# Block 2 of a two-block model on one core: the two output-gate projections of each head pair in seven quarter products

## The chip, the cores and the metric

One core of a Trainium2 chip runs the whole program in one launch. The metric is device time in microseconds (us); lower is better. All data is float32.

## The reference

Two transformer-like blocks run one after the other on 256 tokens of width 1024. The change lies in the second one, in the projection of the normed input `h` and in what follows for two of its parts:

```
h = _rmsnorm(x, norm_g[l]) * (1.0 + scale[:, None, :]) + shift[:, None, :]
p = jnp.einsum('bsd,de->bse', h, w_in[l])
c_val, c_gate, c_og, ts, r_og, g_conv, g_rwkv = jnp.split(p, SPLITS, axis=-1)
y_conv = _conv_branch(c_val, c_gate, c_og, ...)   # ends: silu(u) * silu(og)) @ w_o
y_rwkv = _rwkv7_branch(ts, r_og, ...)             # ends: (o * silu(og)) @ w_o
m = jax.nn.sigmoid(g_conv) * y_conv + jax.nn.sigmoid(g_rwkv) * y_rwkv
x = x + gate[:, None, :] * jnp.einsum('bsd,de->bse', m, w_out[l])
```

`c_og` and `r_og` are the output gates of the convolution and of the recurrence, `g_conv` and `g_rwkv` the branch gates; each is 1024 wide. The recurrence `_rwkv7_scan` runs over 16 heads of width 64.

## The kernel before

**Layout.** `hT` holds the normed input, transposed: 8 tiles `k` of 128 features by 256 tokens. The heads go two by two: 8 pairs of 128 columns. Each pair needs nine projections of 1024x128 weights, and each of these sits in its own slot of SBUF (`slot[w]`, 512 KB a load, issued on SP's queue by `load_projection`): `VAL`, `GATE`, `K_`, `R_`, `V_` (the list `NEXT`), and `OGP`, `ROG`, `GCP`, `GRP` (the list `OWN`: output gate of the convolution, of the recurrence, and the two branch gates). A plain projection (`projection`, L1015) is 8 matmuls of 128x256, accumulated into half a PSUM bank. Successive projections alternate between bank 0 and bank 1, and `read_out` makes each wait until the one two places before it in the same bank has been read.

**Seven products.** The two branch gates of pairs 0 to 6 are computed together (`own_gate_pair`, L1041). The two slots and `hT` are taken as 2x2 blocks (two slots by two halves of the features, and those by two halves of the tokens), and seven products of sums of blocks replace the eight products of blocks. Each is 4 matmuls of 128x128. The sums of `hT`, `bt`, are made once; the sums of the weights are made for each pair by VectorE in four steps of 128x512 (`slice_sum(0)` to `(3)`, L2601, L2604, L2607, L2610); three of them need room of their own (`bs`), one is made in place. The products land as seven quarters in the two banks; ScalarE copies one out (L1792), and VectorE adds the others to it (`first_quarter`, L2615, and `other_quarters`, L2622, L2625, L2627).

**Sections.** Block 2 runs in sections 0 to 8. Section `j` builds the chunk matrices of pair `j` (`grown`, L1186, and `inverted`, L1198 and L1200, five levels each), and at the same time takes the recurrence of pair `j - 1` through its four chunks (`forced`, L1135 and L1137; `solved`, L1145; `outcome`, L1158 to L1172). These are chains of small matmuls in which TensorE and VectorE alternate: `solved(c)` waits until VectorE has copied the result of `forced(c)` out (the copy F{c}, L2554), `outcome(c)` waits for the copy of `solved(c)` (U{c}, L2558), `inverted(l)` waits for the masked copy of `grown(l)` (G{l}, L2572), and the next level waits for VectorE's transpose of `inverted(l)` (L2578; L2585 for the last). To cover these waits, TensorE gets large matmuls between the chains: a generator (`behind`) yields the projections in small steps, and a written table says how many steps each place takes.

```
FILL = (0, 12, 11, 12, 11, 13, 13)
FILL_FIRST = (14, 9, 9, 10, 10, 10, 10)
```

A step is one matmul of 128x256, or two of 128x128 in the seven products. In section `j` of 0 to 6 the steps are, in this order: `NEXT` of pair `j + 1` (40 steps), `OGP` and `ROG` of pair `j` (16), the branch gates of pair `j` (14), 70 in all. The text calls the places fill 0 to fill 6 after their place in the table (fill 0 is empty in `FILL`; the last fill takes what is left, 11 of its 13). Fill 1 stands behind `solved(0)`, fill 2 behind `inverted(1)`, fill 3 behind `inverted(2)`, fill 4 behind `inverted(3)` (in two pieces, with the matmul for the key lengths, `kk.sum`, between them), fill 5 behind `inverted(4)`, fill 6 behind `inverted(5)`.

**VectorE's order.** All of VectorE's work is one list in program order: the copies of the chains, the operands of the next pair (`shift`, L2451; `operand_kp`, L2463; `operand_k`, L2468; `kk_lengths` with its reciprocal, L2474; `operand_b`, from L2478), the 31 taps of the convolution (L2511), the group norm of pair `j - 2` (its reciprocal L2519, in sections 2 to 7), the sums for the branch gates, and the two output gates: `og_silu` (L2589) and `rg_silu` (L2593) multiply a tanh made by ScalarE (L1720) with the projection, which they read from PSUM.

```
e.wait_ge(*act.upto(f"og.th.{j}"))
e.scalar_tensor_tensor(out=OG[:, j, :], in0=OG[:, j, :], scalar=1.0, in1=proj(OGP, j), ...)
```

`shift` of the keys waits for ScalarE's copies of the `K_` projection (L1670, L1672).

Of the kernel before, what the change touches and what calls it, by code (L numbers as in the profile page):

```python
# [110 lines left out]

FILL = (0, 12, 11, 12, 11, 13, 13)
FILL_FIRST = (14, 9, 9, 10, 10, 10, 10)
FILL_LAST = (0, 6, 5, 5, 5, 5, 6)
FILL_END = (0, 3, 3, 2, 3, 3, 3, 3, 3, 3, 3, 3, 2)

# [29 lines left out]
def build(nc, a, out):  # L148

    with ExitStack() as ctx:  # L150
# [869 lines left out]
        def gate_banks_of(q):  # L1020

            return [view3(bank[PLACE[w, q] % 2][:, :], P) for w in (GCP, GRP)]

        def own_gate_pair(e, q):

# [73 lines left out]
        def behind(e, j):  # L1099

            if j < LAST:
                for w in NEXT:
                    yield from projection(e, w, j + 1)
                for w in (OGP, ROG):
                    yield from projection(e, w, j)
                yield from own_gate_pair(e, j)
            elif j == LAST:
                yield from projection(e, OGP, j)
                yield from projection(e, ROG, j)
                yield from layer_sum(e, LNSUM, CU)  # L1110
# [594 lines left out]
        def act_rwkv(e, j):  # L1705
# [65 lines left out]
            if more:  # L1771
                if j:
                    act_pad(e, "v", V_, j + 1)
                half_gate(OGP, OG[:, j, :], "og.th", j)
            if levels:
                inverted(4)
            if more:
                half_gate(ROG, rg[j % 3], "rg.th", j)
            if levels:
                e.wait_ge(*pe.upto(f"tok.{j}"))  # L1780
                e.activation(tokBK[j % 2], chunks(bank[4][:, :]), ACT.Copy).then_inc(*act.step(f"tok.{j}"))
            if last:
                e.wait_ge(*pool.upto("ln.c0"))
                e.activation(lnq[:, 0:4, :], CU[:, 0:4, :], ACT.Square).then_inc(*act.step("ln.sq0"))
                e.wait_ge(*dve.upto("ln.c1"))
                e.activation(lnq[:, 4:8, :], CU[:, 4:8, :], ACT.Square).then_inc(*act.step("ln.sq"))
# [761 lines left out]
        def dve_rwkv(e, j):  # L2548
# [37 lines left out]

            def og_silu():
                e.wait_ge(*act.upto(f"og.th.{j}"))
                e.scalar_tensor_tensor(out=OG[:, j, :], in0=OG[:, j, :], scalar=1.0, in1=proj(OGP, j), op0=ALU.add, op1=ALU.mult).then_inc(*dve.step(f"og.{j}"))  # L2589

            def rg_silu():
                e.wait_ge(*act.upto(f"rg.th.{j}"))
                e.scalar_tensor_tensor(out=rg[j % 3], in0=rg[j % 3], scalar=1.0, in1=proj(ROG, j), op0=ALU.add, op1=ALU.mult).then_inc(*dve.step(f"rg.{j}"))  # L2593

            def slice_sum(k):

# [62 lines left out]
                e.tensor_tensor(Mt[j % 2], chunks(bank[6][:, T:]), each(cst2_of("st")), ALU.mult).then_inc(*dve.step(f"M.{j}"))  # L2659
                turned(1)  # L2660
            if more:
                slice_sum(0)
                dve_decays(e, j + 1)
            if levels:
                taps(e, j, *((23, 28) if not j else (27, CONV2) if more else (22, 27)))
            if j and more:
# [14 lines left out]
            if levels:  # L2681
                turned(2)
            if more:
                slice_sum(1)
                slice_sum(2)
                shift(e, "k", j + 1)
                operand_kp(e, j + 1)
            if j == 0:
                taps(e, j, 28, CONV2)
                join_taps(e, j)  # L2690
                conv_input(e, j + 1)
                taps(e, j + 1, 0, 2)
            elif more:
                taps(e, j + 1, 4, 10)
# [24 lines left out]
            if more:  # L2719
                shift(e, "r", j + 1)  # L2720
                bonus_keys(e, j + 1)
                taps(e, j + 1, *((10, 13) if j else (2, 6)))
                kk_lengths(e, j + 1)
            if last:
                rg_silu()
            if end:
# [10 lines left out]
            if levels:  # L2737
                turned(4)
            if more:
                slice_sum(3)  # L2740
                og_silu()
                operand_b(e, j + 1)
                shift(e, "v", j + 1)
                operand_a(e, j + 1)
                if not chain:
                    taps(e, j + 1, 6, 10)
# [510 lines left out]
        def sp_rwkv(e):  # L3257

            free = {R_: f"down{LATE}", K_: f"down{LATE}", VAL: f"down{BY_PRODUCT - 1}", V_: f"down{BY_PRODUCT - 1}",
                    GATE: "down.p1", ROG: "down.p1", GRP: "down.p5", OGP: "down.p3", GCP: "down.p3"}  # L3260
            summed = {R_: LATE, K_: LATE, VAL: BY_PRODUCT - 1, V_: BY_PRODUCT - 1, GATE: BY_PRODUCT, ROG: DOWN - 2,
                      OGP: BY_PRODUCT, GCP: DOWN - 2}

            def load_projection(w, j):
                e.wait_ge(*pe.upto(f"p{GRP if w == GCP else w}.{j - 1}" if j else free[w]))
# [164 lines left out]
```

## Time and profile before

| what | value |
|---|---|
| median of the timed runs | 1058.26 us (3 runs, 1057.3 to 1058.48) |
| the profiled execution's own time | 1057.9 us |
| span of the profile | 1055.9 us |
| TensorE busy | 1045.8 us |
| VectorE busy | 754.8 us |
| ScalarE busy | 237.4 us |
| sections 2, 3 and 4, from one `forced(0)` to the next | 46.6 us each |

Times in the rows are counted from the start of the span. Float32 matmuls leave two records each, so a row with x24 is 12 matmuls. The time from the start of one row to the start of the next on the same engine is what an instruction takes up; the duration shown is longer, since the end of an instruction lies beside the start of the next.

### The profile page before, as it was taken

To read this page: it belongs to the slowest core of one execution; us is meant where nothing else is said; L and a number is where in the kernel's file an instruction comes from. 1 tells how busy PE (TensorE), PEld (TensorE's weight loads), DVE (VectorE), ACT (ScalarE), POOL (GpSimd) and SP (SyncE) were. 2 spreads that over 40 slices of the span, in tenths; PEclk is the share of its full clock that TensorE was granted. 3 is DMA by queue.
4 is the path that set the end of the run, shared out by engine and by line. 5 is a ranking of instruction groups with operands and counts; after the bars stand their busy time and mean duration, and the time that the engine had idled before them with its cause. 6 is when DMAs were issued, how large, how long until landed. Compare 5 with 4: busy or idle time off the path is not lost.

```text
span 1055.9 us, 21666 instructions
## 1 busy us (share of the span) xinstructions
PE 1045.8 (99%) x8902; PEld 904.3 (86%) x8902; DVE 754.8 (71%) x1714; ACT 237.4 (22%) x630; POOL 121.0 (11%) x166
## 2 busy tenths in 40 slices
PE   9999999999999999999999999999999999999997
PEld 8899899998988499999644988898898989887983
DVE  4488776867743477777757788767878778777875
ACT  4032222213300120011101432323223232324101
POOL 1101000000045121100250000000000000000052
PEclk9999999999999999999999999999999999999999
DMA  8786666552377446554555333333333322161261
GB/s 271 260 308 234 208 197 220 194 186 86 120 228 230 159 71 251 195 190 162 182 194 220 99 102 101 99 103 101 105 102 97 120 82 80 42 241 41 81 160 40
DMA packets 72307, 162.67 MB, mean 154 GB/s; under 512 B 18929, under 2 KB 33169, under 8 KB 72210
## 3 DMA queue, kind: packets, MB, share of 16 engines
q1 hardware_dynamic: 71202, 159.67, 46.1%
q8 instruction: 71, 1.16, 0.4%
q10 hardware_dynamic: 1008, 1.63, 0.4%
q14 instruction: 26, 0.21, 0.1%
HBM read 160.17 MB, written 1.11 MB: 153 GB/s over the span
## 4 chain that ended last, share of the span: by engine, by line
PE 97%; DVE 1%; DMA 1%; issue 0%; ACT 0%; POOL 0%; DVEq 0%; ACTq 0%; POOLq 0%
PE bank L860 27%; PE bank L1015 18%; PE bank L491 13%; PE bank L926 6%; PE bank L1041 4%; PE bank L677 3%; PE bank L792 2%; PE bank L835 2%; PE bank L1186 2%; PE bank L1198 2%; PE bank L1355 2%; PE bank L988 1%; PE bank L1077 1%; PE bank L994 1%; PE bank L569 1%; PE bank L1055 1%
## 5 line engine op out<-in xcount | busy, mean ns | idle before, releaser
L1015 PE MATMUL bank<-hT,slots 128*128 128x256 f32 x896 | 204.5, 382 | 0.0
L1015 PEld LDWEIGHTS bank<-hT,slots 128*128 128x128 f32 x896 | 167.8, 190 | 23.2 <-issue 0.3
L860 PE MATMUL bank<-hT,slots 128*128 128x128 f32 x832 | 103.5, 276 | 0.0
L2511 DVE SCALAR_TENSOR_TENSOR arena<-padA,par,arena 128x256 f32<-128x256 f32 x232 | 102.8, 504 | 0.0
L860 PEld LDWEIGHTS bank<-hT,slots 128*128 128x128 f32 x832 | 97.9, 192 | 0.8 <-issue 0.7
L860 PE MATMUL bank<-arena,slots 128*128 128x128 f32 x768 | 95.6, 275 | 0.0
L860 PEld LDWEIGHTS bank<-arena,slots 128*128 128x128 f32 x768 | 90.9, 192 | 0.5
L491 PE MATMUL bank<-hT,slots 128*128 128x256 f32 x336 | 74.4, 380 | 0.0
L491 PEld LDWEIGHTS bank<-hT,slots 128*128 128x128 f32 x336 | 63.4, 190 | 9.2 <-issue 0.8
L491 PE MATMUL bank<-arena,slots 128*128 128x256 f32 x304 | 66.3, 380 | 0.5 <-DMA slots<-in_w_br 0.5
L491 PEld LDWEIGHTS bank<-arena,slots 128*128 128x128 f32 x304 | 57.5, 190 | 8.8 <-DMA slots<-in_w_br 1.1
L926 PE MATMUL bank<-slots,arena 128*128 128x512 f32 x128 | 55.4, 592 | 0.0
L926 PEld LDWEIGHTS bank<-slots,arena 128*128 128x128 f32 x128 | 24.2, 190 | 30.1 <-issue 25.6
L3052 POOL TENSOR_TENSOR arena<-arena 128x256 f32<-128x256 f32 x8 | 5.8, 728 | 359.8 <-ACT arena L1726 359.8
L860 PE MATMUL bank<-x,arena 128*128 128x128 f32 x352 | 46.5, 275 | 0.0
L860 PE MATMUL bank<-x,slots 128*128 128x128 f32 x352 | 46.5, 275 | 0.0
L860 PEld LDWEIGHTS bank<-x,slots 128*128 128x128 f32 x352 | 42.8, 192 | 0.0
L860 PEld LDWEIGHTS bank<-x,arena 128*128 128x128 f32 x352 | 42.8, 192 | 0.0
L1983 DVE SCALAR_TENSOR_TENSOR adaA<-arena,sc,adaA 128x1024 f32<-128x1024 f32 x24 | 30.7, 1277 | 0.0
L1595 ACT ACTIVATE arena<-bank 128x128 f32<-128x128 f32 x20 | 5.5, 277 | 110.2 <-PE bank L860 98.9
L2981 POOL TENSOR_TENSOR arena<-arena 128x256 f32<-128x256 f32 x8 | 8.0, 1020 | 188.8 <-DMA arena<-cum_scratch 188.8
L2168 DVE SCALAR_TENSOR_TENSOR arena<-arena,bank 128x256 f32<-128x256 f32 x32 | 12.6, 415 | 22.9 <-PE bank L491 15.8
(478 smaller groups left out, 1887.5 us busy)
## 6 DMA issues: line engine op xcount, KB each, us to landing
slots<-in_w_rwkv SPq DMA_DIRECT2D x72, 512.0 KB, 3.6
slots<-in_w_heads SPq DMA_DIRECT2D x64, 512.0 KB, 4.5
slots<-in_w_gu SPq DMA_DIRECT2D x44, 512.0 KB, 4.5
arena<-in_ada_w SPq DMA_DIRECT2D x24, 512.0 KB, 5.5
slots<-in_w_down SPq DMA_DIRECT2D x20, 512.0 KB, 4.4
slots<-in_w_br SPq DMA_DIRECT2D x32, 256.0 KB, 2.8
slots<-in_w_out SPq DMA_DIRECT2D x16, 512.0 KB, 4.2
slots<-in_w_y SPq DMA_DIRECT2D x16, 512.0 KB, 6.5
```

What stands on the lines that cost most here:

```text
L491: end = e.matmul(psum, w[:, k * P:(k + 1) * P], rhs[:, k, :], start=k == 0, stop=k == kt - 1)
L677: end = e.matmul(view3(bank[5][:, t * T:(t + 1) * T], P), hT[:, k, t * P:(t + 1) * P], slots[:, BV:CV + 1, k * P:(k + 1) * P], start=k == ...
L792: return e.matmul(bank[DOWN_BANK[m]][:, :], *sides, start=j == 0, stop=j == OUT_PAIRS - 1)
L835: end = e.matmul(psum[:, tokens(t)], w[:, k * P:(k + 1) * P], hT[:, k, tokens(t)], start=k == 0, stop=k == KT - 1)
L860: end = e.matmul(out, w[:, k * P:(k + 1) * P], rhs[:, k, :], start=k == 0, stop=k == 3)
L926: return e.matmul(bank[DOWN_BANK[m]][:, :], *sides, start=j == 0, stop=j == DOWN - 1)
L1015: end = e.matmul(proj(w, q), slot[w][:, k * P:(k + 1) * P], hT[:, k, :], start=k == 0, stop=k == KT - 1)
L1041: end = e.matmul(out[:, at, :], w[:, k * P:(k + 1) * P], rhs[:, k, :], start=k == 0, stop=k == 3)
L1186: end = e.matmul(bank[2][r, c * CHUNK:(c + 1) * CHUNK], Nt[r, c, :], Xs[r, c, :], start=True, stop=True)
L1198: end = e.matmul(chunks(half(3))[r, c, :], Z[r, c, :], Gs[r, c, :], start=True, stop=True)
L1983: e.scalar_tensor_tensor(out=third, in0=adaW[n % 2], scalar=sc[:, 2 * i + n // 3:2 * i + n // 3 + 1], in1=third, op0=ALU.mult, op1=ALU.add ...
L2511: e.scalar_tensor_tensor(out=o, in0=src, scalar=w, in1=o, op0=ALU.mult, op1=ALU.add).then_inc(*dve.step(f"tap{n}.{q}"))
```

## The change

For pairs 0 to 6 the output gates of the convolution and of the recurrence are no longer two plain projections: `own_output_pair` computes them in seven products, as `own_gate_pair` does for the branch gates. Their weight sums are made by VectorE (`output_sum(0)` to `(3)`) at places where `slice_sum(0)` to `(2)` stood, one of them at a new place behind `dve_decays`; `slice_sum(0)` and `(1)` move behind `kk_lengths`, `(2)` and `(3)` behind `inverted(4)`'s transpose. The quarters are put together by `first_output_sums` and `other_output_sums` in a buffer of their own (`oraw`), ScalarE copies one quarter (`op1`), and makes both tanh from `oraw` after the copy for the tokens; `og_silu` and `rg_silu` read `oraw` and stand together behind the group norm. The tables of steps are changed to the new count, 68. The load of `OGP` waits for the end of the seven products of the pair before.

```diff
-FILL = (0, 12, 11, 12, 11, 13, 13)
-FILL_FIRST = (14, 9, 9, 10, 10, 10, 10)
+FILL = (0, 11, 11, 11, 11, 12, 12)
+FILL_FIRST = (13, 9, 9, 9, 9, 9, 10)
...
+        oraw = carve(4, P)
+        osum = [carve(512) for _ in range(3)]
...
+                elif w in (OGP, ROG) and q < LAST:
+                    e.wait_ge(*dve.upto(f"oq11.{q}" if w == OGP else f"oq1221.{q}"))
...
+        def own_output_pair(e, q):
+
+            one, two = output_banks_of(q)
+            low, high = hT[:, 0:4, :], hT[:, 4:8, :]
+            first, second = (slot[w] for w in (OGP, ROG))
+            parts = ((one, 0, first[:, 0:512], low[:, :, tokens(0)]), (one, 1, first[:, 512:], high[:, :, tokens(0)]), (one, 2, osum[0], bt[1]),
+                     (two, 0, second[:, 0:512], bt[0]), (two, 1, osum[1], bt[2]), (two, 2, osum[2], high[:, :, tokens(1)]), (two, 3, second[:, 512:], bt[3]))
+            for n, (out, at, w, rhs) in enumerate(parts):
...
+                if n == 2:
+                    e.wait_ge(*dve.upto("bt4"))
+                    e.wait_ge(*dve.upto(f"os4.{q}"))
...
+                for k in range(4):
+                    end = e.matmul(out[:, at, :], w[:, k * P:(k + 1) * P], rhs[:, k, :], start=k == 0, stop=k == 3)
+                    if k == 3 and n in (2, 6):
+                        end.then_inc(*pe.step(f"o126.{q}" if n == 2 else f"p{ROG}.{q}"))
+                    if k % 2:
+                        yield
...
-                for w in (OGP, ROG):
-                    yield from projection(e, w, j)
+                yield from own_output_pair(e, j)
                 yield from own_gate_pair(e, j)
...
-                half_gate(OGP, OG[:, j, :], "og.th", j)
+                e.wait_ge(*pe.upto(f"o126.{j}"))
+                e.activation(oraw[:, 1, :], output_banks_of(j)[0][:, 0, :], ACT.Copy).then_inc(*act.step(f"op1.{j}"))
             if levels:
                 inverted(4)
...
+            if more:
+                for n, (to, name) in enumerate(((OG[:, j, :], "og.th"), (rg[j % 3], "rg.th"))):
+                    e.wait_ge(*dve.upto(f"oq1221.{j}"))
+                    e.activation(to, flat(oraw[:, 2 * n:2 * n + 2, :]), ACT.Tanh, scale=0.5).then_inc(*act.step(f"{name}.{j}"))
...
+            def first_output_sums():
+
+                e.wait_ge(*act.upto(f"op1.{j}"))
+                e.tensor_tensor(oraw[:, 0:4:3, :], oraw[:, 1:2, :].to_broadcast([P, 2, P]), output_banks_of(j)[0][:, 1:3, :],
+                                ALU.add).then_inc(*dve.step(f"oq11.{j}"))
+            def other_output_sums():
+
+                two = output_banks_of(j)[1]
+                e.wait_ge(*pe.upto(f"p{ROG}.{j}"))
+                e.wait_ge(*dve.upto(f"oq11.{j}"))
+                e.tensor_tensor(oraw[:, 1:3, :], oraw[:, 3:4, :].to_broadcast([P, 2, P]), two[:, 0:2, :], ALU.add).then_inc(*dve.step(f"ou43.{j}"))
+                e.wait_ge(*dve.upto(f"ou43.{j}"))
+                e.tensor_tensor(oraw[:, 3, :], oraw[:, 2, :], two[:, 0, :], ALU.add).then_inc(*dve.step(f"oq22.{j}"))
+                e.wait_ge(*dve.upto(f"oq22.{j}"))
+                e.tensor_tensor(oraw[:, 1:3, :], oraw[:, 1:3, :], two[:, 2:4, :], ALU.add).then_inc(*dve.step(f"oq1221.{j}"))
...
             if more:
-                slice_sum(0)
+                output_sum(0)
                 dve_decays(e, j + 1)
+                output_sum(1)
...
-                slice_sum(1)
-                slice_sum(2)
+                output_sum(2)
                 shift(e, "k", j + 1)
                 operand_kp(e, j + 1)
+                output_sum(3)
...
                 kk_lengths(e, j + 1)
+                slice_sum(0)
+                slice_sum(1)
...
             if more:
+                first_output_sums()
+                slice_sum(2)
                 slice_sum(3)
-                og_silu()
                 operand_b(e, j + 1)
...
             if more:
-                rg_silu()
+                other_output_sums()
                 operand_r(e, j + 1)
...
                 group_norm(e, g)
             if more:
+                og_silu()
+                rg_silu()
                 taps(e, j + 1, 13 if chain else 10, 18)
```

`output_sum(k)` is `slice_sum(k)` with the slots `OGP` and `ROG` and the buffer `osum`.

On VectorE in section 4, between the transpose of level 2 and the copy F2, these are the rows before (L2604 and L2607 are sums for the branch gates, L2451 the shift of the keys, L2463 `kp`, L2511 taps, L2468 `operand_k`, L2554 the copy F2, L2572 the copy G3):

```order
L2578 STREAM_TRANSPOSE arena<-bank 128x256
L2604 TENSOR_TENSOR slots<-slots 128x512
L2607 TENSOR_TENSOR slots<-slots 128x512
L2451 SCALAR_TENSOR_TENSOR arena<-arena,par 128x256
L2463 TENSOR_TENSOR arena<-arena 128x256
L2511 SCALAR_TENSOR_TENSOR arena<-padA,par,arena 128x256 x6
L2468 TENSOR_TENSOR arena<-arena 128x256
L2554 COPY arena<-bank 128x64
L2572 TENSOR_TENSOR arena<-bank,arena 128x256
```

And these are the rows of the changed kernel at that place (L2641 and L2644 are `output_sum(2)` and `(3)`, L2483 the shift, L2495 `kp`, L2543 taps, L2500 `operand_k`, L2586 the copy F2, L2604 the copy G3):

```order
L2610 STREAM_TRANSPOSE arena<-bank 128x256
L2641 TENSOR_TENSOR arena<-slots 128x512
L2483 SCALAR_TENSOR_TENSOR arena<-arena,par 128x256
L2495 TENSOR_TENSOR arena<-arena 128x256
L2644 TENSOR_TENSOR arena<-slots,arena 128x512
L2543 SCALAR_TENSOR_TENSOR arena<-padA,par,arena 128x256 x6
L2500 TENSOR_TENSOR arena<-arena 128x256
L2586 COPY arena<-bank 128x64
L2604 TENSOR_TENSOR arena<-bank,arena 128x256
```

Two sums stand there in both, but one of them has moved from ahead of the shift of the keys to behind `kp`, and the two are other sums.

On VectorE in section 4, from the transpose of level 4 to the copies U3 and G5, before (L2610 is `slice_sum(3)`, L2589 `og_silu`, L2478 to L2482 `operand_b`, L2451 the shift of the values, L2486 `operand_a`, L2519 the group norm's reciprocal, L2558 the copy U3):

```order
L2578 STREAM_TRANSPOSE arena<-bank 128x256
L2610 TENSOR_TENSOR adaA<-slots 128x512
L2589 SCALAR_TENSOR_TENSOR arena<-arena,bank 128x256
L2478 SCALAR_TENSOR_TENSOR arena<-arena,par 128x256
L2480 SCALAR_TENSOR_TENSOR arena<-arena 128x256
L2482 SCALAR_TENSOR_TENSOR arena<-arena 128x256
L2451 SCALAR_TENSOR_TENSOR arena<-arena,par 128x256
L2486 SCALAR_TENSOR_TENSOR arena<-arena 128x256
L2519 RECIPROCAL arena<-arena 128x256
L2558 COPY arena<-bank 128x64
L2572 TENSOR_TENSOR arena<-bank,arena 128x256
```

The same place of the changed kernel (L2649 is `first_output_sums`, L2675 and L2678 `slice_sum(2)` and `(3)`, L2510 to L2514 `operand_b`, L2590 the copy U3):

```order
L2610 STREAM_TRANSPOSE arena<-bank 128x256
L2649 TENSOR_TENSOR arena<-arena,bank 128x2x128
L2675 TENSOR_TENSOR slots<-slots 128x512
L2678 TENSOR_TENSOR adaA<-slots 128x512
L2510 SCALAR_TENSOR_TENSOR arena<-arena,par 128x256
L2512 SCALAR_TENSOR_TENSOR arena<-arena 128x256
L2514 SCALAR_TENSOR_TENSOR arena<-arena 128x256
L2483 SCALAR_TENSOR_TENSOR arena<-arena,par 128x256
L2518 SCALAR_TENSOR_TENSOR arena<-arena 128x256
L2551 RECIPROCAL arena<-arena 128x256
L2590 COPY arena<-bank 128x64
L2604 TENSOR_TENSOR arena<-bank,arena 128x256
```

`og_silu` has left this place; the first of the output sums and one more weight sum have come in ahead of `operand_b`.

On TensorE in section 4, the end of `inverted(4)`, fill 5 and `solved(3)`, before (L1198 is `inverted`, L1015 plain projections, L1041 the branch gates, L1145 `solved`):

```order
L1198 MATMUL bank3<-arena 64x64 x8
L1015 MATMUL bank0<-hT,slots 128x256 x2
L1015 MATMUL bank1<-hT,slots 128x256 x8
L1041 MATMUL bank0<-hT,slots 128x128 x6
L1145 MATMUL bank7<-arena 64x64 x2
```

And the changed kernel there (L1228 is `inverted`, L1049 the output gates, L1072 the branch gates, L1175 `solved`):

```order
L1228 MATMUL bank3<-arena 64x64 x8
L1049 MATMUL bank0<-slots,arena 128x128 x4
L1049 MATMUL bank1<-slots 128x128 x4
L1049 MATMUL bank1<-slots,arena 128x128 x4
L1049 MATMUL bank1<-hT,arena 128x128 x4
L1049 MATMUL bank1<-slots 128x128 x4
L1072 MATMUL bank0<-hT,slots 128x128 x4
L1175 MATMUL bank7<-arena 64x64 x2
```

Fill 5 held 10 plain steps and 3 steps of products; now it holds 12 steps of products, and the last three quarters of the output gates' first bank and second bank lie in it.

## Rows read from the trace of the kernel before

**Rows 1.** The page, busy time of each engine over the span.

```profile
PE 1045.8 (99%) x8902; PEld 904.3 (86%) x8902; DVE 754.8 (71%) x1714; ACT 237.4 (22%) x630; POOL 121.0 (11%) x166
```

**Rows 2.** Block 2: all that TensorE's matmuls waited for; section 4, busy time by engine.

```profile
PE bank L1041 <- DVE arena L2593: 0.7, 1, 0.7
...
788.00:835.00 47.00, 47.00 (x574) 42.04 (x572) 36.60 (x87) 13.58 (x35) 2.39 (x3) 1.00 0.33 102
```

**Rows 3.** TensorE's timeline, fill 6 of section 3: start, duration, line, shapes, records.

```profile
783.94 2.84 PE L1041 MATMUL bank<-slots 128*128 128x128 f32 x24
786.62 1.06 PE L1041 MATMUL bank<-hT,adaA 128*128 128x128 f32 x8
```

**Rows 4.** Timeline of section 4, VectorE's copy U1; in brackets its idle time before.

```profile
804.21 0.22 DVE L2558 COPY arena<-bank 128x64 f32<-128x64 f32 x1 [0.43 <-PE bank L1145]
```

**Rows 5.** Timeline of section 4, all three engines, fill 3 and the chain behind it.

```profile
806.56 0.65 DVE L2604 TENSOR_TENSOR slots<-slots 128x512 f32<-128x512 f32 x1
806.62 5.35 PE L1015 MATMUL bank<-hT,slots 128*128 128x256 f32 x24
807.25 0.38 ACT L1670 ACTIVATE arena<-bank 128x256 f32<-128x256 f32 x1 [5.47 <-PE bank L1015]
...
807.25 0.69 DVE L2607 TENSOR_TENSOR slots<-slots 128x512 f32<-128x512 f32 x1
808.03 0.48 DVE L2451 SCALAR_TENSOR_TENSOR arena<-arena,par 128x256 f32<-128x256 f32 x1
808.62 0.43 DVE L2463 TENSOR_TENSOR arena<-arena 128x256 f32<-128x256 f32 x1
808.97 2.46 DVE L2511 SCALAR_TENSOR_TENSOR arena<-padA,par,arena 128x256 f32<-128x256 f32 x6
811.34 0.42 DVE L2468 TENSOR_TENSOR arena<-arena 128x256 f32<-128x256 f32 x1
811.90 0.33 PE L1135 MATMUL bank<-arena 64*64 64x64 f32 x4
...
813.34 0.68 PE L1198 MATMUL bank<-arena 64*64 64x64 f32 x16
```

**Rows 6.** Timeline of section 4, fill 5 and the chain behind it.

```profile
822.16 4.58 PE L1015 MATMUL bank<-hT,slots 128*128 128x256 f32 x20
823.33 0.38 ACT L1720 ACTIVATE arena<-bank 128x256 f32<-128x256 f32 x1 [3.80 <-PE bank L1015]
823.74 0.42 DVE L2589 SCALAR_TENSOR_TENSOR arena<-arena,bank 128x256 f32<-128x256 f32 x1 [0.44 <-ACT arena L1720]
824.08 0.48 DVE L2478 SCALAR_TENSOR_TENSOR arena<-arena,par 128x256 f32<-128x256 f32 x1
...
826.13 1.75 DVE L2519 RECIPROCAL arena<-arena 128x256 f32<-128x256 f32 x1
...
828.39 0.22 DVE L2558 COPY arena<-bank 128x64 f32<-128x64 f32 x1 [0.52 <-PE bank L1145]
...
829.46 0.61 PE L1200 MATMUL bank<-arena 64*64 64x32 f32 x16
```

**Rows 7.** Timeline of section 4, VectorE's copy F0; in brackets its idle time before.

```profile
788.88 0.23 DVE L2554 COPY arena<-bank 128x64 f32<-128x64 f32 x1 [0.73 <-PE bank L1137]
```

**Rows 8.** Timeline of section 0, the copies G3, G4, G5 and TensorE's rows behind them.

```profile
630.20 0.41 DVE L2572 TENSOR_TENSOR arena<-bank,arena 128x256 f32<-128x256 f32 x1
...
634.94 1.75 DVE L2474 RECIPROCAL arena<-arena 128x256 f32<-128x256 f32 x1
...
637.08 0.42 DVE L2572 TENSOR_TENSOR arena<-bank,arena 128x256 f32<-128x256 f32 x1 [0.38 <-PE bank L1186]
637.56 0.68 PE L1198 MATMUL bank<-arena 64*64 64x64 f32 x16
...
643.50 0.42 DVE L2572 TENSOR_TENSOR arena<-bank,arena 128x256 f32<-128x256 f32 x1 [0.24 <-PE bank L1186]
...
645.35 2.05 PE L1041 MATMUL bank<-slots 128*128 128x128 f32 x16 [0.72 <-DVE arena L2593]
```

More of the change, by code:

```diff
@@ L1022, in gate_banks_of, with output_banks_of @@
             return [view3(bank[PLACE[w, q] % 2][:, :], P) for w in (GCP, GRP)]
+        def output_banks_of(q):
+            return [view3(bank[PLACE[w, q] % 2][:, :], P) for w in (OGP, ROG)]
+        def own_output_pair(e, q):
[5 more added lines that the diff above has]
+            for n, (out, at, w, rhs) in enumerate(parts):
+                if n == 0:
+                    e.wait_ge(*in_slot[OGP].upto(f"rw{OGP}.{q}"))
+                    read_out(e, PLACE[OGP, q] - 2)
+                if n == 2:
+                    e.wait_ge(*dve.upto("bt4"))
+                    e.wait_ge(*dve.upto(f"os4.{q}"))
+                if n == 3:
+                    read_out(e, PLACE[ROG, q] - 2)
+                for k in range(4):
[4 more added lines that the diff above has]
+                        yield
         def own_gate_pair(e, q):
@@ L1773, in act_rwkv @@
                     act_pad(e, "v", V_, j + 1)
-                half_gate(OGP, OG[:, j, :], "og.th", j)
+                e.wait_ge(*pe.upto(f"o126.{j}"))
+                e.activation(oraw[:, 1, :], output_banks_of(j)[0][:, 0, :], ACT.Copy).then_inc(*act.step(f"op1.{j}"))
             if levels:
                 inverted(4)
-            if more:
-                half_gate(ROG, rg[j % 3], "rg.th", j)
-            if levels:
                 e.wait_ge(*pe.upto(f"tok.{j}"))
                 e.activation(tokBK[j % 2], chunks(bank[4][:, :]), ACT.Copy).then_inc(*act.step(f"tok.{j}"))
+            if more:
+                for n, (to, name) in enumerate(((OG[:, j, :], "og.th"), (rg[j % 3], "rg.th"))):
+                    e.wait_ge(*dve.upto(f"oq1221.{j}"))
+                    e.activation(to, flat(oraw[:, 2 * n:2 * n + 2, :]), ACT.Tanh, scale=0.5).then_inc(*act.step(f"{name}.{j}"))
             if last:
@@ L2588, in og_silu @@
                 e.wait_ge(*act.upto(f"og.th.{j}"))
-                e.scalar_tensor_tensor(out=OG[:, j, :], in0=OG[:, j, :], scalar=1.0, in1=proj(OGP, j), op0=ALU.add, op1=ALU.mult).then_inc(*dve.step(f"og.{j}"))
+                raw = flat(oraw[:, 0:2, :]) if more else proj(OGP, j)
+                e.scalar_tensor_tensor(out=OG[:, j, :], in0=OG[:, j, :], scalar=1.0, in1=raw, op0=ALU.add, op1=ALU.mult).then_inc(*dve.step(f"og.{j}"))
             def rg_silu():
                 e.wait_ge(*act.upto(f"rg.th.{j}"))
-                e.scalar_tensor_tensor(out=rg[j % 3], in0=rg[j % 3], scalar=1.0, in1=proj(ROG, j), op0=ALU.add, op1=ALU.mult).then_inc(*dve.step(f"rg.{j}"))
+                raw = flat(oraw[:, 2:4, :]) if more else proj(ROG, j)
@@ new lines, in rg_silu, with output_sum @@
+                e.scalar_tensor_tensor(out=rg[j % 3], in0=rg[j % 3], scalar=1.0, in1=raw, op0=ALU.add, op1=ALU.mult).then_inc(*dve.step(f"rg.{j}"))
+            def output_sum(k):
+                a11, a12, a21, a22 = (slot[s][:, columns_half(h)] for s in (OGP, ROG) for h in range(2))
+                if k == 0:
+                    e.wait_ge(*in_slot[OGP].upto(f"rw{OGP}.{j}"))
+                    e.wait_ge(*in_slot[ROG].upto(f"rw{ROG}.{j}"))
+                    e.tensor_tensor(osum[1], a11, a21, ALU.subtract).then_inc(*dve.step(f"os3.{j}"))
+                elif k == 1:
+                    e.wait_ge(*dve.upto(f"os3.{j}"))
+                    e.tensor_tensor(a21, a21, a22, ALU.add).then_inc(*dve.step(f"os1.{j}"))
+                elif k == 2:
+                    e.wait_ge(*dve.upto(f"os1.{j}"))
+                    e.tensor_tensor(osum[0], a21, a11, ALU.subtract).then_inc(*dve.step(f"os2.{j}"))
+                else:
+                    e.wait_ge(*dve.upto(f"os2.{j}"))
+                    e.tensor_tensor(osum[2], a12, osum[0], ALU.subtract).then_inc(*dve.step(f"os4.{j}"))
@@ L3262, in sp_rwkv @@
                       OGP: BY_PRODUCT, GCP: DOWN - 2}
+            DONE_BY = {GCP: GRP, OGP: ROG}
             def load_projection(w, j):
-                e.wait_ge(*pe.upto(f"p{GRP if w == GCP else w}.{j - 1}" if j else free[w]))
+                e.wait_ge(*pe.upto(f"p{DONE_BY.get(w, w)}.{j - 1}" if j else free[w]))
                 if j == 0 and w in summed:
```

## The prediction

> **What bounds the kernel now.** I read first which engine is busy: TensorE for 1045.8 of 1055.9 us, VectorE for 754.8 [rows 1]. Then TensorE's waits in block 2: one of 0.7 us in all, in section 0 [rows 2]. In section 4, which stands for sections 2 to 6, TensorE is busy in every one of 47 us at a granted clock of 1.00 (2.4 GHz), VectorE in 36.6 [rows 2]. So work taken from TensorE is time saved, but only as long as VectorE keeps up in the chains. An average of 78% says nothing on that; the timeline says it place by place.
>
> **What TensorE saves.** A record (half a float32 matmul) 128 wide takes (786.62 - 783.94) / 24 = 0.112 us [rows 3]; one 256 wide takes (811.90 - 806.62) / 24 = 0.220 us [rows 5]. Two plain projections are 32 records, 7.04 us; seven products are 56 records, 6.25 us. That is 0.79 us less for each pair, 5.5 us for seven, if nothing waits.
>
> A rule speaks against even this. The Trainium skill, "TensorEngine Tiling (Array Packing)", Instruction Overhead, gives each matmul an overhead of about 60 cycles, so that cutting up a small dimension doesn't pay; for 24 more records at 2.4 GHz that is an estimate of 0.6 us, and 0.2 of the 0.8 us would be left. The rows show no such thing: 0.112 is half of 0.220 within 2%. It has a rival below.
>
> **What VectorE gets.** Per pair four sums of 128x512 (0.65 us shown [rows 5], 0.57 until the next instruction starts, since a row starts about 0.08 before the end of the one ahead: 823.74 with 0.42, then 824.08 [rows 6]; 0.69 when the next one needs the result, 806.56 to 807.25 [rows 5]). Also one `first_output_sums` and three `other_output_sums`, for which the trace has no row of these; the twins for the branch gates have the same shapes. I take 0.34 us, and 0.45 + 0.32 + 0.34 = 1.1 us, as a 256-wide instruction takes 0.34 alone (823.74 to 824.08) and about 0.5 when the next one needs its result (824.08 to 826.13 holds three of the one sort and two of the other [rows 6]); the bounds for the four are 1.1 and 1.9 us. Altogether about 3.8 us. `og_silu` only moves; its reading SBUF instead of PSUM I count as nothing, at most 0.1 us either way.
>
> **Section 4, place by place.** A step is 0.44 us plain and 0.447 in products.
>
> *Fill 1* loses a step, -0.44. VectorE's load here doesn't change.
>
> *Fill 2* keeps 11 steps and VectorE gets `output_sum(1)`, 0.57. It sat idle 0.43 before the copy U1 [rows 4], so U1 comes 0.14 late; `outcome(1)`, which waits for it, has `grown(2)` and a set of products ahead of it. Cost 0. The bound is 0.14.
>
> *Fill 3* loses a step, but VectorE can't use it. Before, ScalarE took the keys' projection at 807.25, 0.63 after the fill's start at 806.62, and the shift of the keys followed at 808.03, as soon as that copy was there [rows 5]. The projection ends with step 24. Fills 1 and 2 held 23 steps, now 22, so it ends one step further into fill 3: the shift starts 1.41 + 0.44 = 1.85 after the fill's start. Ahead of it VectorE now has one sum and then idles; the other one, `output_sum(3)`, stands behind `kp`, where nothing is idle. `operand_k` started at 811.34, so its successor can at 5.06; now 5.06 + 0.44 + 0.57 = 6.07. Then the copy F2 (0.14), and G3 at 6.21, ending at 6.63. TensorE's `inverted(3)` starts 0.06 after G3 ends (637.08 + 0.42, then 637.56 [rows 8]): at 6.69, against 813.34 - 806.62 = 6.72 before [rows 5]. So the fill's gain of 0.44 turns into a wait at `solved(2)` and `inverted(3)`; -0.03 is left.
>
> *Fill 4* has four product steps in place of plain ones: +0.05 with the change of shape.
>
> *Fill 5* goes from 10 plain and 3 product steps (5.74) to 12 product steps (5.37), -0.37. VectorE: before, `og.th` followed OGP's last step, 2 steps into the fill (ScalarE at 1.17), and `og_silu` at 1.58, `operand_b` at 1.92, the reciprocal at 3.97 [rows 6]. Now the third quarter product ends at the same 2 steps; the copy of 128 columns is 0.1 shorter than the tanh, so `first_output_sums` starts at 1.49 (the transpose of level 4 is long done: idle time, where `slice_sum(3)` stood before). Then 0.34, two sums 0.69 + 0.57, and `operand_b` at 3.09, the reciprocal at 5.14. It takes 1.75, about 1.71 until the next: the copy U3 at 6.85, G5 at 6.99, over at 7.41, `inverted(5)` at 7.47. Before it was 829.46 - 822.16 = 7.30 [rows 6]. So instead of -0.37 the stretch costs +0.17 to +0.2; VectorE, which had 0.52 idle before U3 [rows 6], is now 1.1 late there. In section 1 there is no group norm yet, hence no reciprocal: -0.37 is had.
>
> *Fill 6* has 12 steps for 11: +0.45. VectorE: 1.1 and `og_silu` 0.34 more, less 0.73 idle before F0 [rows 7] and the 0.45: F0 comes 0.26 late. `solved(0)` has the products and a turn to tokens ahead of it, about half a microsecond of slack by my reading, so 0; the bound is 0.26. The branch gates' second bank waits for `other_output_sums`, done 1.5 us after the copy of `inverted(5)`, when TensorE is still in the steps before it.
>
> Sum of a section 2 to 6: -0.44 + 0 - 0.03 + 0.05 + 0.18 + 0.45 = +0.21; five are +1.1. Section 1: -0.44 - 0.03 + 0.05 - 0.37 + 0.45 = -0.34.
>
> **Section 0** has shorter fills and no recurrence, and VectorE is its pace already: G3 started at 630.20 with no idle time, `inverted(4)` at 637.56 directly behind G4, and G5 with 0.24 idle [rows 8]. Work -0.79. G3: one step less (-0.44), VectorE's load 0.13 less (the two sums no longer depend on each other): wait +0.31. G4: two sums behind the reciprocal, 0.69 + 0.57 (634.94 + 1.71 + 1.26 = 637.91, against 637.08 less a step): wait +1.26. G5: 0.34 + 0.69 more and `og_silu` 0.34 less, less 0.24 idle, one step less (0.42): wait +0.87. The gate's second bank: before 0.72 of waiting for `rg_silu` [rows 8]; now the three sums end 0.79 later and two more steps cover it, -0.1. Section 0: +1.55.
>
> Total 1.1 - 0.34 + 1.55 = **+2.3 us**. On the profiled execution's own 1057.9 that is 1060.2; the median of the runs shown is 0.36 higher, so the forecast is **1060.6 us**, 0.2% slower: the whole gain of 5.5 us goes into waits of TensorE for VectorE, about 7.8 us of them.
>
> **Rivals.** (a) *VectorE's idle time takes it all in.* It had some 10 of 47 us unused and gets 3.8. Then nothing waits, and the time is 1058.3 - 5.5 = 1052.8. Against it: the idle time lies ahead of copies, not where the sums stand. It comes out faster by over 0.2% (2.1 us) as soon as the waits of sections 1 to 6, which I price at 5 x 0.99 + 0.41 = 5.4, come to less than 1 us. Chance 0.1.
> (b) *Only one of the two waits of a steady section is there*: were U3's missing (the reciprocal gets through, or ScalarE hands its quarter over sooner), 5 x 0.55 less: 1057.9, no difference. Chance 0.23.
> (c) *The late F0 copy decides.* If `solved(0)` has no slack, F0's 0.26 counts in full in six sections, and what is late there reaches the copy U0 and the bonus: +0.3 x 6, 1062.4. It decides if the last taps end more than the slack after `forced(0)`. Chance 0.12.
> (d) *The narrow records cost more*, 0.025 us for each additional one: 0.6 us a pair, of which fill 4 has 0.17 and fill 5 0.43, hidden under U3's wait except in section 1: 5 x 0.17 + 0.6 = 1.5, so 1062.1. So it would go by the page of the Trainium skill named above. Chance 0.03.
> The forecast has 0.52; its own range is 1059.2 to 1062.2.
>
> **How the numbers follow.** Of 12 places with a wait, each is uncertain by 0.15, and they err together (prices of VectorE's instructions 0.03 apart make 0.1 at each): about 1.5 us. With (b) and half of (a) below, and (c) and (d) above, 8 in 10 gives 1055.6 to 1063.3. A measurement of this kernel can tell about 0.2% from no change, that is 1056.1 and 1060.4. Faster: (a) and a part of (b), 0.13. Same: the rest of (b) and the lower part of the forecast, 0.38. Slower: its upper part with (c) and (d), 0.49.
>
> **What the new profile would show.** TensorE's waits in block 2 go from one to a dozen or more, by name at `solved` (L1175) or `inverted` (L1228) behind fill 3, and at `outcome(3)` in sections 2 to 6 for the copy U3; VectorE has no idle time before F2 and U3 and about 1 us before `first_output_sums`; records of 128 stay at 0.112. From one `forced(0)` to the next, sections 2 to 6 take 46.8 instead of 46.6 us, section 0 1.5 us more, section 1 0.3 less. A section of 45.8 us would show me wrong, and so would VectorE idle before U3.

## The result, and the profile after

The changed kernel takes 1060.71 us (median of 8 runs, 1060.22 to 1062.81), the kernel before 1057.94 (8 runs, 1056.96 to 1058.48): ratio 1.0028, 95% interval 1.0019 to 1.0037. It is slower by 2.8 us, and the forecast was 2.3 slower. The profiled execution took 1060.8 us with a span of 1058.8, against 1055.9. Of these 2.9 us, 0.37 lie ahead of section 0's chains (the first low-rank matmuls, L978, start at 596.21; before, as L976, at 595.84), 0.34 of them in the first 9 us, where the input arrives later; over the traces of all kernels here that start lies anywhere from 595.5 to 596.9. The other 2.55 lie between it and the start of section 7, and they are what the change costs.

The page of the changed kernel, busy time:

```profile
PE 1044.4 (99%) x9070; PEld 908.1 (86%) x9070; DVE 777.4 (73%) x1770; ACT 240.3 (23%) x637; POOL 120.6 (11%) x166
```

TensorE is 99% busy in both profiles [rows 1], and busy for 1.4 us less, not 5.5: a busy share says nothing on short waits, since the modelled end of a matmul reaches into the gap behind it. All that the view of waits lists for its matmuls in block 2 (us in total, times, longest):

```profile
PE bank L1228 <- DVE arena L2604: 1.7, 2, 1.3
PE bank L1197 <- DVE arena L2590: 1.4, 5, 0.3
PE bank L1230 <- DVE arena L2604: 0.8, 1, 0.8
PE bank L1072 <- DVE arena L2661: 0.4, 1, 0.4
```

One wait has become nine [rows 2], each for VectorE: `inverted` for the copies G3, G4 and G5 (L2604), `outcome(3)` five times for the copy U3 (L2590), the gates' second bank for `other_output_sums` (L2661). Section 4, the timeline of the three engines, fill 3 and the chain behind it (start, duration, line, in brackets idle time before):

```profile
808.31 0.65 DVE L2641 TENSOR_TENSOR arena<-slots 128x512 f32<-128x512 f32 x1
808.37 4.91 PE L1019 MATMUL bank<-hT,slots 128*128 128x256 f32 x22
809.44 0.39 ACT L1700 ACTIVATE arena<-bank 128x256 f32<-128x256 f32 x1 [5.47 <-PE bank L1019]
810.22 0.48 DVE L2483 SCALAR_TENSOR_TENSOR arena<-arena,par 128x256 f32<-128x256 f32 x1 [1.26 <-ACT arena L1702]
811.15 0.69 DVE L2644 TENSOR_TENSOR arena<-slots,arena 128x512 f32<-128x512 f32 x1
813.22 0.33 PE L1165 MATMUL bank<-arena 64*64 64x64 f32 x4
813.96 0.63 PE L990 MATMUL bank<-arena 64*64 64x64 f32 x16
814.13 0.42 DVE L2500 TENSOR_TENSOR arena<-arena 128x256 f32<-128x256 f32 x1
814.46 0.22 DVE L2586 COPY arena<-bank 128x64 f32<-128x64 f32 x1
814.60 0.41 DVE L2604 TENSOR_TENSOR arena<-bank,arena 128x256 f32<-128x256 f32 x1
814.74 0.33 PE L1175 MATMUL bank<-arena 64*64 64x64 f32 x4
815.07 0.68 PE L1228 MATMUL bank<-arena 64*64 64x64 f32 x16
```

Against [rows 5]: ScalarE takes the keys' projection 1.07 us after the fill's start, where it was 0.63. VectorE does one sum and sits idle for 1.26 us; the other sum stands behind `kp`, and from there to the copy F2 there is no idle time. `inverted(3)` (L1228) starts 815.07 - 808.37 = 6.70 us after the fill's start, before it was 6.72, although the fill is a step shorter. The wait shows in no bracket and in no line of the view of waits: `solved(2)` (L1175) starts 1.21 us after `forced(2)` before, and 814.74 - 813.22 = 1.52 now, but the row ahead of it (L990) is drawn to 814.59, and what remains is 0.15. `inverted(3)` comes another 0.10 late behind it (0.33 after `solved(2)`, 0.23 before), so the wait is 0.41 in all.

Fill 5 and its chain in the same section:

```profile
823.95 1.16 PE L1049 MATMUL bank<-slots,arena 128*128 128x128 f32 x8
824.95 1.06 PE L1049 MATMUL bank<-slots 128*128 128x128 f32 x8
825.14 0.28 ACT L1805 ACTIVATE arena<-bank 128x128 f32<-128x128 f32 x1 [4.53 <-PE bank L1049]
825.45 0.42 DVE L2649 TENSOR_TENSOR arena<-arena,bank 128x256 f32<-128x256 f32 x1 [0.94 <-ACT arena L1805]
825.79 0.69 DVE L2675 TENSOR_TENSOR slots<-slots 128x512 f32<-128x512 f32 x1
829.17 1.75 DVE L2551 RECIPROCAL arena<-arena 128x256 f32<-128x256 f32 x1
829.50 0.33 PE L1175 MATMUL bank<-arena 64*64 64x64 f32 x4
830.83 0.16 DVE L2590 COPY arena<-bank 128x64 f32<-128x64 f32 x1
830.91 0.41 DVE L2604 TENSOR_TENSOR arena<-bank,arena 128x256 f32<-128x256 f32 x1
831.05 0.33 PE L1197 MATMUL bank<-arena 64*64 64x64 f32 x4 [0.28 <-DVE arena L2590]
831.44 0.61 PE L1230 MATMUL bank<-arena 64*64 64x32 f32 x16
```

Against [rows 6]: VectorE is idle 0.94 us until ScalarE's copy of the quarter (L1805) is there; then come two weight sums, and the reciprocal (L2551) ends only after `solved(3)` (829.50). So the copy U3 starts 1.33 us after `solved(3)`, where it started 0.38 after it (828.39, L1145 at 828.01): it is 0.95 late, `outcome(3)` waits, and `inverted(5)` (L1230) starts 831.44 - 823.95 = 7.49 after the fill's start, 7.30 before.

The waits in section 0, against [rows 8]:

```profile
630.48 0.68 PE L1228 MATMUL bank<-arena 64*64 64x64 f32 x16 [0.41 <-DVE arena L2604]
...
638.17 0.68 PE L1228 MATMUL bank<-arena 64*64 64x64 f32 x16 [1.28 <-DVE arena L2604]
...
645.00 0.66 PE L1230 MATMUL bank<-arena 64*64 64x32 f32 x16 [0.85 <-DVE arena L2604]
645.58 1.16 PE L1072 MATMUL bank<-slots 128*128 128x128 f32 x8
647.15 2.05 PE L1072 MATMUL bank<-slots 128*128 128x128 f32 x16 [0.41 <-DVE arena L2661]
```

And the starts of `forced(0)` in sections 1, 2, 4 and 5:

```profile
650.91 0.33 PE L1167 MATMUL bank<-arena 64*64 64x64 f32 x4
...
696.99 0.33 PE L1167 MATMUL bank<-arena 64*64 64x64 f32 x4
...
790.69 0.33 PE L1167 MATMUL bank<-arena 64*64 64x64 f32 x4
...
837.54 0.33 PE L1167 MATMUL bank<-arena 64*64 64x64 f32 x4
```

Section 4 takes 46.85 us, as do 2, 3, 5 and 6 (46.6 before); section 1 takes 46.08 (46.17 before).

### The profile page after: what moved, and what is told of

The parts are those of the page before. It is cut to its first block, busy times and chain, and to the rows that moved or that the text cites. A ratio compares the mean times of both kernels' runs of the same rounds, so it can differ in the third digit from the quotient of the medians.

```text
span 1058.8 us, 22079 instructions
## 1 busy us (share of the span) xinstructions
PE 1044.4 (99%) x9070; PEld 908.1 (86%) x9070; DVE 777.4 (73%) x1770; ACT 240.3 (23%) x637; POOL 120.6 (11%) x166
## 4 chain that ended last, share of the span: by engine, by line
PE 90%; DVE 7%; ACT 1%; issue 1%; DMA 1%; POOL 0%; DVEq 0%; ACTq 0%; POOLq 0%
PE bank L862 27%; PE bank L493 13%; PE bank L1019 11%; PE bank L928 6%; PE bank L1072 4%; PE bank L679 3%; PE bank L794 2%; PE bank L837 2%; PE bank L1049 2%; PE bank L1228 2%; DVE arena L2543 2%; PE bank L1385 2%; PE bank L1108 1%; PE bank L1216 1%; PE bank L990 1%
## 5 line engine op out<-in xcount | busy, mean ns | idle before, releaser
L1019 PE MATMUL bank<-hT,slots 128*128 128x256 f32 x672 | 153.8, 381 | 0.0
L1019 PEld LDWEIGHTS bank<-hT,slots 128*128 128x128 f32 x672 | 126.0, 190 | 17.1
L2543 DVE SCALAR_TENSOR_TENSOR arena<-padA,par,arena 128x256 f32<-128x256 f32 x232 | 102.9, 505 | 0.0
L862 PEld LDWEIGHTS bank<-hT,slots 128*128 128x128 f32 x832 | 97.9, 192 | 0.8 <-issue 0.7
L493 PE MATMUL bank<-hT,slots 128*128 128x256 f32 x336 | 74.4, 380 | 0.0
L493 PEld LDWEIGHTS bank<-hT,slots 128*128 128x128 f32 x336 | 63.4, 190 | 9.2 <-issue 0.8
```

The source lines that it names most:

```text
L493: end = e.matmul(psum, w[:, k * P:(k + 1) * P], rhs[:, k, :], start=k == 0, stop=k == kt - 1)
L862: end = e.matmul(out, w[:, k * P:(k + 1) * P], rhs[:, k, :], start=k == 0, stop=k == 3)
L1019: end = e.matmul(proj(w, q), slot[w][:, k * P:(k + 1) * P], hT[:, k, :], start=k == 0, stop=k == KT - 1)
L2543: e.scalar_tensor_tensor(out=o, in0=src, scalar=w, in1=o, op0=ALU.mult, op1=ALU.add).then_inc(*dve.step(f"tap{n}.{q}"))
```

## The experiments

Theory: the waits come from the **places** at which VectorE's additional work stands, three of them: behind `kp`, ahead of `operand_b`, and section 0. The rival says that VectorE's **load** as such is the bound. Every edit is made to the changed kernel, but for the last two, which start from the version with both moves and the one in section 0. Every kernel was timed in five rounds beside the kernel before; its ratios have an interval of about 0.1% to either side. The changed kernel itself was not timed again beside them, so a difference to its 1060.71 is good to about 1 us. The length of a section in the traces tells more: where the same instructions stand in the same order, it repeats to 0.02 us.

**The fourth output sum ahead of the shift of the keys**

```diff
                 output_sum(2)
+                output_sum(3)
                 shift(e, "k", j + 1)
                 operand_kp(e, j + 1)
-                output_sum(3)
```

> The last of the four output sums moves ahead of the shift of the keys, into VectorE's idle time of 1.26 us there (sections 1 to 6; section 0 has no such idle time, there it costs 0.1). Theory of places: F2 and G3 come 0.57 sooner, TensorE no longer waits behind fill 3 (inverted(3) 6.28 to 6.3 us after the start of fill 3, now 6.70), so 6 x 0.41 - 0.1 = 2.3 us less than the changed kernel: 1058.4. Theory of VectorE's total load: the same instructions in the list, so no difference: 1060.7. A third theory, that the late keys' projection and not the sum behind it makes the wait: G3 is then as late as before, 1060.7, with VectorE idle right ahead of the shift still 0.6 us or less and inverted(3) unmoved.

Measured: 1058.13 us, before 1057.89, ratio 1.0002 (0.9993 to 1.0011), so 2.6 us below the changed kernel. Its timeline in section 4:

```profile
806.92 4.91 PE L1019 MATMUL bank<-hT,slots 128*128 128x256 f32 x22
808.77 0.48 DVE L2483 SCALAR_TENSOR_TENSOR arena<-arena,par 128x256 f32<-128x256 f32 x1 [0.53 <-ACT arena L1702]
812.41 0.22 DVE L2586 COPY arena<-bank 128x64 f32<-128x64 f32 x1
813.21 0.68 PE L1228 MATMUL bank<-arena 64*64 64x64 f32 x16
```

The shift of the keys starts 1.85 us after the fill's start as it did, but VectorE's idle time ahead of it is 0.53 instead of 1.26, and `inverted(3)` comes after 6.29 us. Sections 2 to 6 take 46.43 us instead of 46.85, section 1 45.67 instead of 46.08. So the late keys alone make no wait; the sum behind them does.

**One weight sum ahead of the first output sums**

```diff
-                first_output_sums()
                 slice_sum(2)
+                first_output_sums()
                 slice_sum(3)
```

> slice_sum(2) moves ahead of first_output_sums, into VectorE's idle time of 0.94 us while ScalarE's copy of a quarter isn't there yet. Theory of places: in sections 2 to 6 the copy U3 comes 0.6 to 0.7 sooner and inverted(5) starts about 6.95 instead of 7.49 us after the start of fill 5: 5 x 0.55 = 2.7 us less than the changed kernel, 1058.0; nothing in section 1, whose list has no reciprocal there, and nothing in section 0, where the copy is there already. Theory of total load: 1060.7.

Measured: 1057.88 us, ratio 1.0001 (0.9992 to 1.001), 2.8 us below the changed kernel.

```profile
822.64 1.16 PE L1049 MATMUL bank<-slots,arena 128*128 128x128 f32 x8
824.14 0.42 DVE L2649 TENSOR_TENSOR arena<-arena,bank 128x256 f32<-128x256 f32 x1 [0.36 <-ACT arena L1805]
827.13 1.74 DVE L2551 RECIPROCAL arena<-arena 128x256 f32<-128x256 f32 x1
828.79 0.16 DVE L2590 COPY arena<-bank 128x64 f32<-128x64 f32 x1
829.64 0.61 PE L1230 MATMUL bank<-arena 64*64 64x32 f32 x16
```

`first_output_sums` (L2649) waits 0.36 instead of 0.94, the reciprocal starts 0.73 sooner after the fill's start, and `inverted(5)` after 7.00 us instead of 7.49. Sections 2 to 6 take 46.35 us.

**Both moves**

> Both moves. Theory of places: the two waits lie in different stretches, so their gains add: 2.3 + 2.7 = 5.0 less than the changed kernel, 1055.7, that is 2.2 us faster than the kernel before; a section 2 to 6 takes 45.9 us (46.85 in the changed kernel, 46.61 before). If VectorE's load as such is the bound, what is cleared at one place comes back at the next (the copy F0 is already late), and the time stays near 1060.

Measured: 1055.57 us, ratio 0.9978 (0.997 to 0.9987). The gains add up to within 0.3 us (2.6 + 2.8, and 5.1 together), and a section of 2 to 6 takes 45.95 us. The rival is out: nothing came back at another place (section 0 takes 54.69 us, as in the changed kernel).

**Only the table: one step from the last fill to fill 3**

```diff
-FILL = (0, 11, 11, 11, 11, 12, 12)
+FILL = (0, 11, 11, 12, 11, 12, 11)
```

> Only the table: FILL = (0, 11, 11, 12, 11, 12, 12) with the last fill taking what is left, 11 steps; one step moves from fill 6 to fill 3. Theory of places: fill 3 hides the step in its wait (inverted(3) still 6.7 us after the start of fill 3), fill 6 gets 0.45 shorter; VectorE then has F0 0.64 late, of which solved(0) has 0.5 of slack: 0.25 to 0.45 a section gained, six sections, so 1058.0 to 1059.2. If TensorE's work and not VectorE's list sets the pace behind fill 3, the order of the steps makes no difference: 1060.7.

Measured: 1057.42 us, ratio 0.9995 (0.9986 to 1.0004), 3.3 us below the changed kernel; 1.5 to 2.7 were expected. The places held (`inverted(3)` 6.72 after the start of fill 3), but I had overlooked fill 5:

```profile
822.00 0.71 PE L1049 MATMUL bank<-slots,arena 128*128 128x128 f32 x4
823.06 0.42 DVE L2649 TENSOR_TENSOR arena<-arena,bank 128x256 f32<-128x256 f32 x1 [0.49 <-ACT arena L1805]
829.04 0.61 PE L1230 MATMUL bank<-arena 64*64 64x32 f32 x16
```

With a step more ahead of fill 5, the third quarter product ends a step sooner in it; `first_output_sums` starts 1.06 us after the fill's start instead of 1.50, and `inverted(5)` after 7.04 instead of 7.49. That is 0.45 of the 0.54 us by which the section gets shorter; fill 6 gives back 0.2 and not 0.45, for `other_output_sums` comes too late for it, and the late copy F0 costs 0.1 behind it.

**The same useless instruction at two places**

`extra` is a free stretch of `adaA`; the addition feeds nothing. In the first kernel it stands behind `output_sum(2)`, in the second behind `slice_sum(3)`:

```diff
+                e.tensor_tensor(extra, osum[1], osum[1], ALU.add).then_inc(*dve.step(f"extra.{j}"))
```

> The changed kernel with one more 128x512 addition for VectorE in each of sections 0 to 6, of no use to the output, behind output_sum(2), where VectorE idles 1.26 us (not in section 0). Theory of places: nothing in sections 1 to 6, 0.6 us in section 0, so 1061.3. Theory of total load: 0.57 in every section, 4 us, 1064.7.

> The same additional instruction, the same number of times, behind slice_sum(3) and ahead of operand_b, where VectorE is late. Theory of places: 0.57 to 0.6 in sections 2 to 6 and in section 0, and nothing in section 1, where 0.63 us of idle time stand before the copy U3: 3.5 us, 1064.2. Theory of total load: the same as extra_idle, whatever that gives.

Measured: 1061.15 us in the idle time (ratio 1.003, 1.0019 to 1.0041), 1064.85 ahead of `operand_b` (ratio 1.006, 1.0048 to 1.0073), beside the same runs of the kernel before, 1058.32. TensorE's waits in block 2, of the first and then of the second kernel (one line has been added, so U3 is L2591, G3 to G5 are L2605; the gates' second bank waits 0.4 in both, as it did, and is left out):

```profile
PE bank L1229 <- DVE arena L2605: 2.3, 2, 1.3
PE bank L1198 <- DVE arena L2591: 1.4, 5, 0.3
PE bank L1231 <- DVE arena L2605: 0.9, 1, 0.9
```

```profile
PE bank L1198 <- DVE arena L2591: 4.4, 5, 0.9
PE bank L1229 <- DVE arena L2605: 1.7, 2, 1.3
PE bank L1231 <- DVE arena L2605: 1.4, 1, 1.4
PE bank L1176 <- DVE arena L2587: 0.5, 1, 0.5
```

In the idle time, seven instructions of 0.6 us cost 0.6 us once, in section 0, where VectorE has no such idle time (55.30 us instead of 54.70; the waits of L1229 grow from 1.7 to 2.3); the medians differ by 0.4. Sections 1 to 6 are not longer by 0.01. Ahead of `operand_b`, `outcome(3)`'s five waits grow from 1.4 to 4.4, G5's in section 0 from 0.8 to 1.4, one of 0.5 for the copy F2 (L2587) is new in section 6 (there `kp`, L2496, waits 0.46 for ScalarE, as in none of sections 1 to 5), and section 1 doesn't change (46.07 us). The same work costs nothing or its full length, by its place.

**Section 0: two weight sums into idle time**

```diff
+            if j == 0:
+                slice_sum(0)
             if levels:
                 e.wait_ge(*pe.upto(f"bonus.{j}"))
...
+            if j == 0:
+                slice_sum(1)
...
                 kk_lengths(e, j + 1)
-                slice_sum(0)
-                slice_sum(1)
+                if j:
+                    slice_sum(0)
+                    slice_sum(1)
```

The second stands behind the taps that precede the copy G1.

> The changed kernel, and in section 0 alone slice_sum(0) stands ahead of the bonus (0.92 us idle there) and slice_sum(1) ahead of the copy G1 (0.90 us idle), instead of behind the reciprocal. Theory of places: TensorE's wait of 1.28 us for G4 in section 0 goes, all else stays: 1059.4. If section 0 is held up by VectorE's load altogether, the waits for G3 or G5 grow instead: 1060.2 to 1060.7.

> Both moves of the earlier run and the one of section 0. Theory of places: 1055.6 less 1.3 is 1054.3, 3.6 us or 0.34% below the kernel before; TensorE's remaining waits in block 2 are those for G3, G5 and the gates' second bank in section 0, 1.7 us. Theory of total load: no better than 1055.6.

Measured: on the changed kernel alone 1059.28 us (ratio 1.0011, 1.0002 to 1.002), with both moves 1054.59 (ratio 0.9964, 0.9951 to 0.9978). What TensorE still waits for in block 2 with all three:

```profile
PE bank L1230 <- DVE arena L2604: 0.7, 1, 0.7
PE bank L1228 <- DVE arena L2604: 0.5, 1, 0.5
PE bank L1072 <- DVE arena L2661: 0.4, 1, 0.4
```

Three waits in section 0; G4's is gone, U3's five are gone. Section 0 takes 53.48 us in the first of the two kernels and 53.49 in the second, instead of 54.70.

**The table that helped, where its waits are gone**

> The kernel of both_section0 with the table that gained 3.3 us on the changed kernel, FILL = (0, 11, 11, 12, 11, 12, 11). Theory of places: a step gains in fill 3 only where it fills a wait. The waits behind fills 3 and 5 are gone here, so the step costs its 0.44 in fill 3, gives 0.45 back in fill 6, and there the copy F0 and the gates' second bank are too late for the shorter fill, 0.2 to 0.3 a section: 1.2 to 1.8 us slower than both_section0 (1054.6), 1055.8 to 1056.4. If that table is better as such, it gains again: 1051 to 1053.

Measured: 1056.05 us, ratio 0.9984 (0.9975 to 0.9993), 1.5 us slower than without it; a section of 2 to 6 takes 46.27 instead of 45.95, section 1 45.89 instead of 45.66. The table that gained 3.3 us was no better table; it filled waits that another order avoids.

**A third weight sum in section 0**

```diff
+            if j == 0:
+                slice_sum(2)
             if levels:
                 turned(4)
             if more:
-                slice_sum(2)
+                if j:
+                    slice_sum(2)
                 first_output_sums()
```

> The kernel of both_section0, and in section 0 slice_sum(2) too stands earlier, ahead of the transpose of level 4, where VectorE idles 0.78 us. Theory of places: the wait for G5 in section 0 falls from 0.85 to 0.25: 1054.0. It is the version with the fewest waits; 0.6 us is just what one comparison can tell.

Measured: 1053.98 us, before 1057.99, ratio 0.9956 (0.9943 to 0.9968). The wait for G5 is no longer among TensorE's waits. This version beats both kernels: by 4.0 us the one before, by 6.7 the changed one. That it is better than both moves with the one in section 0 (1054.59) by 0.6 lies within what the two intervals allow; what shows it is the wait that is gone and the length of section 0, 52.88 us instead of 53.49. The kernel before had one listed wait, of 0.72 us, to lose [rows 2], so the 4.0 us come from the products.

## Why the prediction was right, and where it was off

The likeliest case came out, with the time 0.1 us from the forecast. That close, it is luck: the comparison is good to 1 us to either side, the 0.37 ahead of the chains are in no forecast, and in block 2 the sum was off by +0.25 in section 1, by -0.13 in section 0 and by 0.15 in sections 2 to 6 together. What was right is where the waits come from, and the size of the two in a steady section.

- *The price of the products.* It held in the new buffers too: inside fill 5, eight records take 825.84 - 824.95 = 0.89 us, 0.111 each. All 48 took 829.50 - 823.95 = 5.55 us; by rival (d), with 0.43 more in this fill, they would have taken 5.37 + 0.43 = 5.80. So rival (d) is out. With it goes one reading of the Trainium skill, "TensorEngine Tiling (Array Packing)", Instruction Overhead, which gives each matmul about 60 cycles: taken as a cost on top of 128 columns, the trace doesn't agree with it. What the sum left out is the change of shape behind the 64-wide matmuls: the first eight records take 1.00 us (823.95 to 824.95). So fill 5 is 0.30 shorter than before and not 0.37, which stays under U3's wait in sections 2 to 6. Where both waits are gone, a section takes 45.95 us, 0.65 less than before: that, and not 0.79, is what the products save.
- *Fill 3.* Forecast: `inverted(3)` 6.69 after the fill's start; measured 6.70. That it is the place of `output_sum(3)` was tested: moving it gave 2.6 us for the 2.3 worked out. The sign that the prediction named was not there, though: no wait behind fill 3 is listed, and the view has nine waits, not a dozen or more. With the six of 0.4 us that only the starts of the rows show, there are fifteen.
- *Fill 5.* Forecast: U3 at 6.85, `inverted(5)` at 7.47; measured 6.88 and 7.49. Tested: 2.8 us for the 2.7 worked out.
- *Sections 2 to 6*: +0.21 each was forecast, +0.24 measured.
- *Section 1*: -0.34 forecast, -0.09 measured. This step was off. Section 0 ends with eight taps of pair 1 instead of five, and so the copy F0 comes 0.46 late there, not 0.26; `solved(0)` in section 1 starts at 652.12, 1.21 us after `forced(0)`, against 1.10 in section 4. What the prediction called a bound of rival (c) did decide once, in this section, for about 0.15. Fill 5 is shorter by 0.30, not 0.37, for 0.07. The last 0.03 are fill 1, shorter by 0.42 instead of 0.44, and the stretch from fill 3 to `inverted(3)`, shorter by 0.02 instead of 0.03.
- *Section 0*: +1.55 forecast, +1.42 measured (53.28 us before, 54.70 after, from the start of the low-rank matmuls at 595.84 and 596.21). The additional waits for G3, G4 and G5 were worked out as 0.31, 1.26 and 0.87. From the start of `grown` to that of `inverted` it is 1.55, 2.43 and 2.00 us, and was 1.25, 1.21 and 1.21: +0.30, +1.22 and +0.79 (the brackets, 0.41, 1.28 and 0.85, count from the modelled end of the row ahead). The gates' second bank was forecast to wait 0.1 less, and that holds, though its bracket falls from 0.72 to 0.41. Before, it started 645.35 - 643.98 = 1.37 us after `inverted(5)`:

```profile
643.98 0.65 PE L1200 MATMUL bank<-arena 64*64 64x32 f32 x16
```

  Now it starts 647.15 - 645.00 = 2.15 us after it, with eight records (0.90) in between, so 0.12 less. The 0.13 by which section 0 is below the forecast are nearly all in G4 and G5.
- *Rivals.* (a) VectorE's idle time doesn't take in the work; the useless instruction shows why: it costs less than 0.01 us a section in one idle gap and 0.6 us ahead of a copy that TensorE waits for. (b) Both waits of a steady section are there. (c) In sections 2 to 6, F0 is 0.19 late and `solved(0)` starts at its usual 1.10: nothing.

So the change as written saves TensorE some 0.65 us of work for each pair and gives it back as waits, with interest. The seven products as such are worth it: with VectorE's sums at other places, and not one instruction less, the same kernel is 0.4% faster than the one before.

## What to carry to other kernels

A quarter of an engine's time being free does not mean that there is room for more work: look at what stands between two of its copies that another engine waits for, and put the new instruction right ahead of one of its own waits that ends late for another reason. Here that decided between 0.3% slower and 0.4% faster, with the same instructions.

A fill that gets shorter is a gain only where the other engine has idle time left in the same stretch. And a table of fills belongs to the order it was fitted to: re-fit it after the order, not in its stead.

Walk one steady section with start-to-start times of rows (not durations, not busy shares, and not the brackets alone); the two ends here that set the waits came out to 0.03 us.

## What the runs showed of the hardware

An independent instruction on VectorE starts about 0.08 us before the shown end of the one ahead (825.45 with 0.42, then 825.79), and so it is behind a reciprocal: 829.17 with 1.75 us, the copy U3 at 830.83, 1.66 later.

TensorE's brackets show less than it waited: `solved(2)` starts 0.31 us later behind `forced(2)` than before and has none, and `outcome(3)` starts 0.91 us after the row ahead of it (L996 at 830.14, then 831.05) instead of 0.47 (L994 at 828.64, then 829.11) and has one of 0.28 for these 0.44. Such waits left its busy share at 99%.

A 128-wide float32 record takes 0.11 us in a run of its kind. In fill 5, the first eight behind 64-wide matmuls take 1.00 us, the next eight 0.89.
